# Latent attention: the key norm's sum of squares in one matmul over 96 rows

## The chip, the cores and the metric

The kernel is one program on one core of a Trainium2 chip. The metric is the time of one execution in device microseconds (us), the median of several executions. TensorE (PE, with its weight loads as PEld), VectorE (DVE), ScalarE (ACT), GpSimd (POOL) and the DMA queue of SyncE (SP) run side by side and wait for one another by semaphores.

## The reference

The input `x` (256 tokens by 1024) passes two layers of a first block and then two layers of a second one. The change lies in the second block, in the keys of its latent attention, twice, once per layer. Cut to that:

```python
c_q, c_kv, k_r, q_d, k_d, v_d = jnp.split(h @ w_in[l], split_at, axis=-1)
kv = (rmsnorm(c_kv, g_ckv) @ w_ukv).reshape(B, S, MLA_HEADS, MLA_NOPE + MLA_V)
k_nope, v = kv[..., :MLA_NOPE], kv[..., MLA_NOPE:]
k_rope = jnp.broadcast_to(k_rope_in[:, :, None, :], (B, S, MLA_HEADS, MLA_ROPE))
k = jnp.concatenate([k_nope, k_rope], axis=-1)
k = rmsnorm(k, g_kn)          # over 96 features: 64 of the head, 32 shared by all heads
k = jnp.concatenate([k[..., :MLA_NOPE], apply_rope_2(k[..., MLA_NOPE:], cos, sin)], axis=-1)
return dense_attention(q * (MLA_QK ** -0.5), k, v)
```

There are 8 heads. A key has 64 features of its own head and 32 (the rope part) that all heads share, and it is divided by the root of the mean square over all 96. In the same layer 8 heads of a dilated attention work on `q_d`, `k_d`, `v_d`; then come the output projection and a feed-forward part.

## The kernel before

All activations lie with features on the partitions and tokens along the free dimension, T = 256 tokens. Weights are streamed in pieces of up to 1 MB: SP loads a piece into one of three `raw` buffers, ACT copies it to a rounded high part `wh`, DVE subtracts to get the low part `wl` (`split`), and each product of the large matmuls (`gemm`, L1316) is taken three times, high by high, high by low, low by high.

The order of the work is set by hand. `plan_program` runs through the whole computation once in Python and writes a list of steps. Each engine's program walks that list and issues its own part of each step (the functions of the same name in the tensor, scalar, vector and gpsimd programs). Buffers come from pools handed out first in, first out: 8 PSUM banks, 8 temporaries `tmp` of 128x512, and a few smaller ones. A buffer that is given back carries the events after which it may be written, and whoever takes it next waits for them. So a buffer that is held longer leaves fewer for the others, and the order of the pool decides who waits for whom.

In a layer of the second block, the steps around the change are these.

- `lora1` (planned at L1057, ACT at L1659): ACT squares the three banks with the latent query and the latent key (`sq3`). The third bank also holds, in rows 64 to 95, the raw rope part of the keys; ACT squares that into `sqkr` (L1665, 32x256), and copies it scaled by the gain into `xg`. After it ACT has the next weight split.
- `lora2`: TensorE sums the squares by matmuls with a matrix of ones, ACT forms the reciprocal roots, and DVE and ACT write the normalised latents `cqn` and `ckn` in five steps, each through a temporary `u`. At its end DVE rotates the rope part of the keys into `krr`.
- Then six pieces of the dilated heads' projections (`dil_piece`), two of the queries (`queries`), each with head norms `hn1` and `hn2`, and from the fourth on, between them, the dilated attention itself (`heads("d")`: scores `sc2`, `exp2`, `wt2`, transposes `turn2`, values `val2`).
- `mla_proj` then projects the keys in four head pairs, hp = 0 to 3. For one pair `mla_k1` makes the 64 own features of both heads in one bank (12 matmuls, two heads side by side in the free dimension, 2 x 256), and ACT squares rows 0 to 63 into a temporary `sq`. One turn of the loop later, `mla_k2` (L1472) sums the squares over the features: one matmul with ones over rows 0 to 63 of `sq` (64x512), and two over rows 64 to 95 of `sqkr` (32x256), one for each head, all adding up in one bank `nb`. ACT takes logarithm and exponential (`rsqrt`), DVE multiplies into `k2` in two instructions (L1935, L1937), and the scores of these two heads may start.
- The steps of `mla_proj` are woven with those of the dilated heads (pair 0) and of the latent heads (pairs 1 to 3), so on TensorE a pair's `mla_k2` stands between scores and the next pair's `mla_k1`.

The trace gives matmuls of all small kinds the line L1351. A matmul on 4-byte numbers has two records in the trace, so the one over 64x512 is "x2", and the two over 32x256 are "x4". In shapes such as 64*96, the first number is the rows used (the contraction), the second the columns.

Of the kernel before, what the change touches and what calls it, by code (L numbers as in the profile page):

```python
# [11 lines left out]
ACT = mybir.ActivationFunctionType  # L12
# [4 lines left out]
T = 256  # L17
# [137 lines left out]
class Memory:  # L155
    def __init__(self, nc, banks):
# [78 lines left out]
        r2 = area(reg_off)  # L235
# [6 lines left out]
        self.kd = r2("kd", [P, 4, T])  # L242
        self.vd = r2("vd", [P, 2, 512])
        self.krr = r2("krr", [96, T])
        self.sqkr = r2("sqkr", [96, T])
        assert r2.end() <= b1_off
        rx = area(ctx_off)
        self.E2 = [rx(f"e2_{i}", [P, 512]) for i in range(2)]
# [10 lines left out]
class Plan:  # L259
# [15 lines left out]
    def ev(self, sem, by=1):  # L275
        self.count[sem] = self.count.get(sem, 0) + by
        return Ev(sem, self.count[sem])

    def step(self, name, **data):
        self.order.append((name, {k: as_now(v) for k, v in data.items()}))  # L280
# [96 lines left out]
def plan_program(M, pieces):  # L377
    p = Plan(M, pieces)
    ev, step, banks, tmps, stats, take = p.ev, p.step, p.banks, p.tmps, p.stats, p.take
# [57 lines left out]
    t_c, t_cs, z = ev("ld_c", 16), ev("csil"), ev("zero")  # L437
# [489 lines left out]
    for s in "cx":  # L927
        hd = ffn1(0, s, ht[s], ffn_step)
        nn, t = ffn_down("dn1", 0, s, hd, mvec(0, s, 5), t_mod[(0, 2)], [], True)
# [86 lines left out]
    n, t = ffn_down("dn1", 1, "x", hd, mvec(1, "x", 5), t_mod[(1, 2)], [], True)  # L1016
# [6 lines left out]
    for l in range(2):  # L1023
        a = H["x"]
        toks = n.finish(M.V(("an", l)), None, a, hfree["x"], [t, t_vec])
        rf = list(region_free)
        dil = {}

        def dil_piece(j):
# [11 lines left out]
            else:  # L1041
# [10 lines left out]
        f = take(("in2", l, 2))  # L1052
        bc = banks.get()
        tc = p.gemm(f, 8, 160, [(0, P, 0, bc), (64, 96, T, bc)], a, toks)
        sq3, xg = [tmps.get() for _ in range(3)], tmps.get()
        a3, k_sq, z, k_g = [ev("lsq") for _ in range(3)], ev("lsq"), ev("zero"), ev("lsq")
        step("lora1", l=l, bk=(ba, bb, bc), tk=(ta, tb, tc), sq3=sq3, sq_free=[q.free for q in sq3], xg=xg,  # L1057
             xg_free=xg.free, rf=rf, a3=a3, k_sq=k_sq, z=z, k_g=k_g)
        dil_piece(0)
        nq, nkv, br, rq, rk = banks.get(), banks.get(), banks.get(), None, None  # L1060
        tq, tkv, t_sw = ev("mm"), ev("mm"), ev("mm")
# [5 lines left out]
        r_free = (rq.free, rk.free)  # L1067
# [26 lines left out]
        cq_toks, ck_toks, t_krr = c_toks[0:3], c_toks[3:5], t_kr[2]  # L1094
# [47 lines left out]
            yield  # L1142

        def k_part(hp, f):
            b, sq = banks.get(), tmps.get()
            t, x = ev("mm"), ev("ksq")
            step("mla_k1", hp=hp, f=f, b=b, free=b.free, ck_toks=ck_toks, sq=sq, sq_free=sq.free, t=t, x=x)

            def rest():
                nb, r = banks.get(), tmps.get()  # L1150
                tn, t_l, t_r, o1, o2 = ev("mm"), ev("ln"), ev("rs"), ev("k2"), ev("k2")
                step("mla_k2", l=l, hp=hp, b=b, sq=sq, x=x, k_sq=k_sq, nb=nb, nb_free=nb.free, r=r, r_free=r.free,
                     t_krr=t_krr, tn=tn, t_l=t_l, t_r=t_r, o1=o1, o2=o2, rf=rf)
                tmps.give(sq, tn)
                banks.give(nb, t_l)
                banks.give(b, o1)
                tmps.give(r, o2)
                k_toks.append(o2)
            return rest, t
# [78 lines left out]
        bk = []  # L1238
# [12 lines left out]
        for ch in range(2):  # L1251
            f = take(("out2", l, 0, ch))
            for i in range(2):
                tk = p.gemm(f, 4, 512, [(P * (2 * i + j), P, T * j, bk[2 * ch + i]) for j in range(2)], H["c"],
                            mix_toks, first=False, done=i == 1)
                t = add_resid(s, bk[2 * ch + i], tk, 2 * ch + i, None, None, [])
# [58 lines left out]
def tensor_program(pe, on, M, plan):  # L1315
# [34 lines left out]
    def mm(out, lhsT, rhs, start, stop):  # L1350
        return pe.matmul(out, lhsT, rhs, start=start, stop=stop, skip_group_check=True)  # L1351
# [117 lines left out]
                ins = mm(o, whi[:, k, c], M.ckn[1][:, k, :], False, k == 1)  # L1469
        ins.then_inc(*on.inc(t))  # L1470

    def mla_k2(sq, x, k_sq, nb, nb_free, tn, **_):  # L1472
        on.wait_ge(x, nb_free, k_sq)
        mm(nb.t[0:96, :], M.ones[0:64, 0:96], sq.t[0:64, :], True, False)
        for i in range(2):
            ins = mm(nb.t[0:96, T * i:T * i + T], M.ones[64:96, 0:96], M.sqkr[64:96, :], False, True)
        ins.then_inc(*on.inc(tn))

    def sc2(mla, h, b, free, ready, t, **_):
        on.wait_ge(ready, free)  # L1480
# [30 lines left out]
def scalar_program(act, on, M, plan, io):  # L1511
# [3 lines left out]
    def fn(out, in_, func, scale=1.0, bias=0.0, accum=None):  # L1515
        if func in (ACT.Ln, ACT.Exp):
            if table[0] != LOG_SET:
                act.preload_act_table_set(LOG_SET)
            table[0] = LOG_SET
        elif func not in (ACT.Copy, ACT.Identity, ACT.Square):  # L1520
            table[0] = func
        if accum is None:
            return act.activation(out, in_, func, bias=bias, scale=scale)  # L1523
        return act.activation(out, in_, func, bias=bias, scale=scale, accum_out=accum)
# [131 lines left out]
        on.wait_ge(t, b1_free)  # L1656
        fn(M.bias[:, h, :], o.t[:, :], ACT.Copy).then_inc(*on.inc(x))

    def lora1(l, bk, tk, sq3, sq_free, xg, xg_free, rf, a3, k_sq, z, k_g, **_):  # L1659
        for i, n in enumerate((512, 512, T)):  # L1660
            on.wait_ge(tk[i], sq_free[i])
            fn(sq3[i].t[:, 0:n], bk[i].t[:, 0:n], ACT.Square).then_inc(*on.inc(a3[i]))
        on.wait_ge(rf)
        kr = bk[2].t[64:96, T:2 * T]
        fn(M.sqkr[64:96, :], kr, ACT.Square).then_inc(*on.inc(k_sq))  # L1665
        on.wait_ge(xg_free)
        fn(xg.t[64:96, 0:T], kr, ACT.Copy, scale=M.vcol(("gmk", l), 0, 64, 96)).then_inc(*on.inc(k_g))

# [19 lines left out]
    def mla_k2(nb, r, r_free, tn, t_l, t_r, **_):  # L1688
        on.wait_ge(tn, r_free)
        rsqrt(r, nb.t[0:96, :], 512, 1.0 / 96, t_l, t_r)  # L1690
# [552 lines left out]
```

## Time and profile before

| | |
|---|---|
| median of 3 runs | 1815.62 us (1813.46 to 1820.35) |
| the profiled execution | 1810.96 us |
| its span, first to last instruction | 1809.2 us |
| its mean granted TensorE clock | 0.975 of full speed |
| TensorE busy, matmuls | 1702.9 us, 94% |
| TensorE busy, weight loads | 1534.6 us, 85% |
| VectorE busy | 1062.7 us, 59% |
| ScalarE busy | 886.4 us, 49% |
| GpSimd busy | 192.7 us, 11% |
| DMA | 299.12 MB, mean 165 GB/s |

Busy shares are means over the span. The second block's two layers begin at about 1070 us and 1440 us, and each has its latent keys about 90 to 135 us later. Start times in the rows are us from the start of the span. "idle before" in brackets is the time that the engine stood before the row, with the instruction that ended it.

### The profile page before, as it was taken

The numbers are of one execution on the slowest core, as the hardware profiler recorded it, in microseconds if no ns is written. First come the engines' busy times: TensorE is split into PE (matmuls) and PEld (weight loads), VectorE is DVE, ScalarE is ACT, GpSimd is POOL, SyncE is SP. The second block draws the span as 40 slices with busy tenths as digits, with TensorE's granted clock in tenths as the row PEclk, the third lists the DMA queues.
The fourth block names the chain that finished last, engine by engine and source line by source line (L and its number), as shares of the span: only waits on it lengthen the run. The fifth ranks groups of instructions, "written<-read, shape, count | busy, mean of one in ns | idle before, by whom it ended". The sixth has DMA issues, their size and how long they took to land. (4 is left out here: it accounts for less than half of the span.)

```text
span 1809.2 us, 30326 instructions
## 1 busy us (share of the span) xinstructions
PE 1702.9 (94%) x12896; PEld 1534.6 (85%) x12896; DVE 1062.7 (59%) x1472; ACT 886.4 (49%) x1190; POOL 192.7 (11%) x138
## 2 busy tenths in 40 slices
PE   5899988999999999988999999998999999989999
PEld 2777657999999999956899989667999996679999
DVE  2498556544455445976644455746776457457763
ACT  3334556544354434555544445645654456455552
POOL 1140000122002210300122100000111000000110
PEclk7999989999999999999999999999999999899999
DMA  8234546456546544472465443303455443025552
GB/s 365 94 140 163 210 175 233 187 211 240 189 153 216 186 175 158 171 263 79 142 217 186 176 155 129 115 24 110 173 186 193 171 143 117 3 91 191 188 195 103
DMA packets 45110, 299.12 MB, mean 165 GB/s; under 512 B 5216, under 2 KB 7360, under 8 KB 11696
## 3 DMA queue, kind: packets, MB, share of 16 engines
q1 hardware_dynamic: 44304, 295.65, 45.6%
q8 instruction: 102, 1.67, 0.4%
q0 software_dynamic: 240, 0.79, 0.1%
q10 hardware_dynamic: 432, 0.75, 0.1%
q14 instruction: 32, 0.26, 0.0%
HBM read 296.10 MB, written 1.06 MB: 164 GB/s over the span
## 5 line engine op out<-in xcount | busy, mean ns | idle before, releaser
L1747 DVE TENSOR_TENSOR wl<-raw,wh 128x2048 fp32r<-128x2048 f32 (+3 forms) x236 | 529.0, 2242 | 520.9 <-ACT wh L1523 470.4
L1523 ACT ACTIVATE wh<-raw 128x2048 fp32r<-128x2048 f32 (+3 forms) x236 | 437.1, 1855 | 260.7 <-PE bank L1331 163.9
L1326 PE MATMUL bank<-hx_hi,wh 128*128 128x256 f32 x1920 | 548.1, 285 | 16.3 <-ACT hx_hi L1523 9.7
L1329 PE MATMUL bank<-hx_hi,wl 128*128 128x256 f32 x1920 | 539.2, 281 | 2.9 <-DVE wl L1747 2.9
L1331 PE MATMUL bank<-hx_lo,wh 128*128 128x256 f32 x1920 | 539.1, 281 | 0.0
L1326 PEld LDWEIGHTS bank<-hx_hi,wh 128*128 128x128 f32 x1920 | 362.8, 189 | 24.2 <-issue 19.3
L1329 PEld LDWEIGHTS bank<-hx_hi,wl 128*128 128x128 f32 x1920 | 362.4, 189 | 8.3 <-DVE wl L1747 4.2
L1331 PEld LDWEIGHTS bank<-hx_lo,wh 128*128 128x128 f32 x1920 | 362.6, 189 | 0.4 <-DVE hx_lo L1739 0.2
L1326 PE MATMUL bank<-hid_hi,wh 128*128 128x256 f32 x880 | 246.0, 280 | 0.0
L1329 PE MATMUL bank<-hid_hi,wl 128*128 128x256 f32 x880 | 245.7, 279 | 0.0
L1331 PE MATMUL bank<-hid_lo,wh 128*128 128x256 f32 x880 | 245.7, 279 | 0.0
L1326 PE MATMUL bank<-hc_hi,wh 128*128 128x256 f32 x752 | 218.1, 290 | 6.5 <-issue 3.0
L1329 PE MATMUL bank<-hc_hi,wl 128*128 128x256 f32 x752 | 214.1, 285 | 7.0 <-DVE wl L1747 7.0
L1331 PE MATMUL bank<-hc_lo,wh 128*128 128x256 f32 x752 | 213.9, 284 | 1.5 <-DVE hc_lo L1854 0.8
L1331 PEld LDWEIGHTS bank<-hid_lo,wh 128*128 128x128 f32 x880 | 165.2, 188 | 0.0
L1326 PEld LDWEIGHTS bank<-hid_hi,wh 128*128 128x128 f32 x880 | 165.1, 188 | 0.0
L1329 PEld LDWEIGHTS bank<-hid_hi,wl 128*128 128x128 f32 x880 | 164.9, 187 | 0.0
L1326 PEld LDWEIGHTS bank<-hc_hi,wh 128*128 128x128 f32 x752 | 145.2, 193 | 19.8 <-issue 19.5
L1329 PEld LDWEIGHTS bank<-hc_hi,wl 128*128 128x128 f32 x752 | 145.0, 193 | 8.2 <-DVE wl L1747 7.8
L1523 ACT ACTIVATE tmp<-bank,vec 128x256 f32<-128x256 f32 (+3 forms) x188 | 105.8, 586 | 92.7 <-PE bank L1331 52.4
L1331 PEld LDWEIGHTS bank<-hc_lo,wh 128*128 128x128 f32 x752 | 145.4, 193 | 2.1 <-DVE hc_lo L1854 1.0
L2029 POOL TENSOR_TENSOR hid_lo<-tmp,hid_hi 128x512 fp32r<-128x512 f32 x33 | 91.6, 2777 | 350.0 <-ACT hid_hi L1523 350.0
(211 smaller groups left out, 1982.2 us busy)
## 6 DMA issues: line engine op xcount, KB each, us to landing
raw<-in_wts SPq DMA_DIRECT2D x258, 1024.0 KB, 4.8
raw<-in_wts SPq DMA_DIRECT2D x20, 768.0 KB, 4.0
raw<-in_wts SPq DMA_DIRECT2D x4, 576.0 KB, 3.5
tmp<-tscr SPq DMA_DIRECT2D x16, 128.0 KB, 4.2
raw<-in_wts SPq DMA_DIRECT2D x2, 640.0 KB, 3.8
xTc<-in_ctxT SPq DMA_DIRECT2D x1, 1024.0 KB, 10.8
xTx<-in_xT SPq DMA_DIRECT2D x1, 1024.0 KB, 8.6
out_x<-xTx POOLq DMA_DIRECT2D x3, 256.0 KB, 5.5
```

The costliest lines, as they stand in the source:

```text
L1326: pe.matmul(out, hi[:, k, c:c + m], x_hi, start=first and k == 0 and o == 0, stop=False, skip_group_check=True)
L1329: pe.matmul(out, lo[:, k, c:c + m], x_hi, start=False, stop=False, skip_group_check=True)
L1331: ins = pe.matmul(out, hi[:, k, c:c + m], x_lo, start=False, stop=last and k == nk - 1, skip_group_check=True)
L1523: return act.activation(out, in_, func, bias=bias, scale=scale)
L1747: tt(M.wl[k][:, 0:ne], M.raw[f["r"]][:, 0:ne], M.wh[k][:, 0:ne].bitcast(F32), ALU.subtract).then_inc(*on.inc(f["tlo"]))
L2029: tt(lo, y.t[:, :], hi.bitcast(F32), ALU.subtract).then_inc(*on.inc(t[1]))
```

## The change

The squares of the rope part are no longer in a tensor of their own. In `lora1` two temporaries, `kq`, are taken from the pool, and ACT writes the squares twice into each, once per head of a pair, into rows 64 to 95 (32x512, the source read twice by a broadcast). The four head pairs use these two buffers in turn as their `sq`: ACT still writes the own squares into rows 0 to 63, and one matmul over rows 0 to 95 (96x512) replaces the three. The buffers stay out of the pool until the third and fourth pair are done with them. A pair's own squares wait for the matmul of the pair two before.

```diff
-        self.sqkr = r2("sqkr", [96, T])
...
         sq3, xg = [tmps.get() for _ in range(3)], tmps.get()
-        a3, k_sq, z, k_g = [ev("lsq") for _ in range(3)], ev("lsq"), ev("zero"), ev("lsq")
+        kq = [tmps.get() for _ in range(2)]
+        a3, k_sq, z, k_g = [ev("lsq") for _ in range(3)], [ev("lsq"), ev("lsq")], ev("zero"), ev("lsq")
...
+        kq_use = [[t] for t in k_sq]
...
-            b, sq = banks.get(), tmps.get()
+            b, sq = banks.get(), kq[hp % 2]
...
-            step("mla_k1", hp=hp, f=f, b=b, free=b.free, ck_toks=ck_toks, sq=sq, sq_free=sq.free, t=t, x=x)
+            step("mla_k1", hp=hp, f=f, b=b, free=b.free, ck_toks=ck_toks, sq=sq, sq_free=kq_use[hp % 2], t=t, x=x)
...
-                tmps.give(sq, tn)
+                kq_use[hp % 2] = [tn]
+                if hp > 1:
+                    tmps.give(sq, tn)
...
-    def mla_k2(sq, x, k_sq, nb, nb_free, tn, **_):
-        on.wait_ge(x, nb_free, k_sq)
-        mm(nb.t[0:96, :], M.ones[0:64, 0:96], sq.t[0:64, :], True, False)
-        for i in range(2):
-            ins = mm(nb.t[0:96, T * i:T * i + T], M.ones[64:96, 0:96], M.sqkr[64:96, :], False, True)
-        ins.then_inc(*on.inc(tn))
+    def mla_k2(sq, x, nb, nb_free, tn, **_):
+        on.wait_ge(x, nb_free)
+        mm(nb.t[0:96, :], M.ones[0:96, 0:96], sq.t[0:96, :], True, True).then_inc(*on.inc(tn))
...
-        on.wait_ge(rf)
         kr = bk[2].t[64:96, T:2 * T]
-        fn(M.sqkr[64:96, :], kr, ACT.Square).then_inc(*on.inc(k_sq))
+        for i in range(2):
+            on.wait_ge(kq_free[i])
+            fn(kq[i].t[64:96, :].rearrange("p (a t) -> p a t", a=2), kr.unsqueeze(1).to_broadcast([32, 2, T]),
+               ACT.Square).then_inc(*on.inc(k_sq[i]))
```

No instruction changes its place against the others on any engine: eight times two matmuls go from TensorE, and twice one ACT instruction becomes two. The numbers behind the names of buffers are those of the tensors; without `sqkr` those of later tensors are one less (`e_0_124` is `e_0_123`), and the temporaries rotate in another order. `cst` holds the matrix of ones, and L1354 is the line that was L1351.

TensorE, first layer, pair 0, behind the scores of a dilated head (`kd`,`qd`), before:

```order
L1351 MATMUL bank<-pT_0_126,vd 64x256 x2
L1494 MATMUL bank<-cst,e_0_124 128x128 x4
L1351 MATMUL bank<-kd,qd 128x256 x2
L1351 MATMUL bank<-tmp_84,cst 96x512
L1351 MATMUL bank<-sqkr,cst 96x256 x2
L1351 MATMUL bank<-ckn_hi,wh_58 128x256
```

and of the changed kernel:

```order
L1354 MATMUL bank<-pT_0_125,vd 64x256 x2
L1494 MATMUL bank<-cst,e_0_123 128x128 x4
L1354 MATMUL bank<-kd,qd 128x256 x2
L1354 MATMUL bank<-tmp_83,cst 96x512
L1354 MATMUL bank<-ckn_hi,wh_58 128x256
```

The two matmuls on `sqkr` are gone, all else stands as it stood. An order row gives the shape of the output, so that the matmul on `tmp` reads 96x512 in both, with 64 rows of input before and 96 now.

TensorE, first layer, pair 1, behind the scores of the first two latent heads (`k_117`,`q_116`), before:

```order
L1351 MATMUL bank<-pT_0_126,vd 64x256 x2
L1351 MATMUL bank<-k_117,q_116 128x256 x4
L1351 MATMUL bank<-tmp_82,cst 96x512
L1351 MATMUL bank<-sqkr,cst 96x256 x2
L1351 MATMUL bank<-ckn_hi,wh_58 128x256
```

and of the changed kernel:

```order
L1354 MATMUL bank<-pT_0_125,vd 64x256 x2
L1354 MATMUL bank<-k_117,q_116 128x256 x4
L1354 MATMUL bank<-tmp_79,cst 96x512
L1354 MATMUL bank<-ckn_hi,wh_58 128x256
L1354 MATMUL bank<-ckn_hi,wl_61 128x256
```

Here the matmul stands behind one over 96 rows, and pairs 2 and 3 read the same but for what is next to them.

ACT, first layer, `lora1`, from the squares of the three banks to the square of the next projection, before:

```order
L1523 ACTIVATE tmp_84<-bank 128x512
L1523 ACTIVATE tmp_80<-bank 128x256
L1523 ACTIVATE sqkr<-bank 32x256
L1523 ACTIVATE tmp_82<-bank,vec 32x256
L1523 ACTIVATE wh_58<-raw_55 128x2048
L1523 ACTIVATE tmp_83<-bank 128x512
```

and of the changed kernel:

```order
L1523 ACTIVATE tmp_84<-bank 128x512
L1523 ACTIVATE tmp_80<-bank 128x256
L1523 ACTIVATE tmp_83<-bank 32x512
L1523 ACTIVATE tmp_79<-bank 32x512
L1523 ACTIVATE tmp_82<-bank,vec 32x256
L1523 ACTIVATE wh_58<-raw_55 128x2048
L1523 ACTIVATE tmp_81<-bank 128x512
```

`tmp_83` and `tmp_79` are the two `kq` buffers. They are the ones that the next head norm took before, and it takes the two behind them now.

## Rows read from the trace of the kernel before

**Rows 1.** The page, busy time of the engines.

```profile
PE 1702.9 (94%) x12896; PEld 1534.6 (85%) x12896; DVE 1062.7 (59%) x1472; ACT 886.4 (49%) x1190; POOL 192.7 (11%) x138
```

**Rows 2.** Groups by line and form, all of the span: the squares' matmuls, ACT's square.

```profile
L1351 PE MATMUL bank<-sqkr,cst 32*96 32x256 f32 x32 | 12.5, 525 | 0.0
L1351 PE MATMUL bank<-tmp,cst 64*96 64x512 f32 x16 | 10.8, 758 | 0.0
L1523 ACT ACTIVATE tmp<-bank 64x512 f32<-64x512 f32 x8 | 4.7, 587 | 5.5 <-PE bank L1351 5.5
```

**Rows 3.** Waits of TensorE, 1075 to 1235: us in total, times, longest.

```profile
PE bank L1494 <- DVE e L1735: 3.6, 2, 2.9
PE bank L1351 <- DVE k L1937: 1.4, 1, 1.4
```

**Rows 4.** Timeline of TensorE, pair 1: start, us, engine, line, what, count.

```profile
1187.23 1.10 PE L1351 MATMUL bank<-tmp,cst 64*96 64x512 f32 x2
1188.26 1.10 PE L1351 MATMUL bank<-sqkr,cst 32*96 32x256 f32 x4
1189.28 0.38 PE L1351 MATMUL bank<-ckn_hi,wh 128*128 128x256 f32 x1
...
1192.29 1.13 PE L1351 MATMUL bank<-k,q 96*128 96x256 f32 x4 [1.37 <-DVE k L1937]
```

**Rows 5.** Timeline of TensorE, scores of a dilated head, then query norms.

```profile
1134.10 1.13 PE L1351 MATMUL bank<-kd,qd 64*128 64x256 f32 x4
1135.16 3.67 PE L1351 MATMUL bank<-tmp,cst 96*96 96x512 f32 x8
1138.27 0.69 PE L1343 MATMUL bank<-wh,hx_hi 128*128 128x256 f32 x1
```

**Rows 6.** Timeline of TensorE, pair 0.

```profile
1169.63 0.48 PE L1351 MATMUL bank<-kd,qd 64*128 64x256 f32 x1
1169.64 0.84 PE L1351 MATMUL bank<-tmp,cst 64*96 64x512 f32 x1
...
1171.29 2.02 PE L1351 MATMUL bank<-sqkr,cst 32*96 32x256 f32 x4
1173.24 0.58 PE L1351 MATMUL bank<-ckn_hi,wh 128*128 128x256 f32 x1
```

**Rows 7.** Windows: us, busy of each engine (count), granted clock, DMA share, GB/s.

```profile
1170.20:1176.80 6.60, 6.60 (x23) 4.44 (x21) 3.98 (x9) 3.87 (x10) 0.00 (x0) 0.50 0.01 1
...
1194.00:1200.60 6.60, 6.60 (x23) 4.81 (x22) 2.28 (x5) 2.23 (x6) 0.00 (x0) 0.50 0.00 0
```

**Rows 8.** Timeline of ACT, pair 1.

```profile
1188.29 0.20 ACT L1524 ACTIVATION_READ_ACCUMULATOR e<-bank,st 128x1 f32 x1
1189.39 0.69 ACT L1523 ACTIVATE tmp<-bank,vec 96x512 f32<-96x512 f32 x1 [0.91 <-PE bank L1351]
```

**Rows 9.** Timeline of TensorE and DVE, pair 2.

```profile
1193.35 1.51 PE L1351 MATMUL bank<-tmp,cst 64*96 64x512 f32 x2
...
1196.73 0.58 PE L1351 MATMUL bank<-ckn_hi,wh 128*128 128x256 f32 x1
...
1199.00 0.68 DVE L1937 TENSOR_TENSOR k<-tmp,krr 32x512 f32<-32x512 f32 x1
...
1199.46 1.05 PE L1494 MATMUL bank<-cst,e 128*128 128x128 f32 x4
```

**Rows 10.** Timeline of ACT, DVE and TensorE, `lora1`.

```profile
1093.46 0.38 ACT L1523 ACTIVATE sqkr<-bank 32x256 f32<-32x256 f32 x1
...
1096.36 2.29 DVE L1747 TENSOR_TENSOR wl<-raw,wh 128x2048 fp32r<-128x2048 f32 x1 [4.41 <-ACT wh L1523]
...
1101.01 0.28 PE L1329 MATMUL bank<-hx_hi,wl 128*128 128x256 f32 x1
```

**Rows 11.** Timeline of ACT and DVE, end of `lora2` and the next head norms.

```profile
1108.73 0.42 DVE L1930 TENSOR_TENSOR krr<-krr,tmp 32x256 f32<-32x256 f32 x1
...
1110.82 0.68 ACT L1523 ACTIVATE tmp<-bank,vec 128x512 f32<-128x512 f32 x1
```

More of the change, by code:

```diff
@@ L1055, in plan_program @@
         sq3, xg = [tmps.get() for _ in range(3)], tmps.get()
-        a3, k_sq, z, k_g = [ev("lsq") for _ in range(3)], ev("lsq"), ev("zero"), ev("lsq")
+        kq = [tmps.get() for _ in range(2)]
+        a3, k_sq, z, k_g = [ev("lsq") for _ in range(3)], [ev("lsq"), ev("lsq")], ev("zero"), ev("lsq")
         step("lora1", l=l, bk=(ba, bb, bc), tk=(ta, tb, tc), sq3=sq3, sq_free=[q.free for q in sq3], xg=xg,
-             xg_free=xg.free, rf=rf, a3=a3, k_sq=k_sq, z=z, k_g=k_g)
+             xg_free=xg.free, a3=a3, kq=kq, kq_free=[q.free for q in kq], k_sq=k_sq, z=z, k_g=k_g)
+        kq_use = [[t] for t in k_sq]
         dil_piece(0)
@@ L1151, in rest @@
                 tn, t_l, t_r, o1, o2 = ev("mm"), ev("ln"), ev("rs"), ev("k2"), ev("k2")
-                step("mla_k2", l=l, hp=hp, b=b, sq=sq, x=x, k_sq=k_sq, nb=nb, nb_free=nb.free, r=r, r_free=r.free,
+                step("mla_k2", l=l, hp=hp, b=b, sq=sq, x=x, nb=nb, nb_free=nb.free, r=r, r_free=r.free,
                      t_krr=t_krr, tn=tn, t_l=t_l, t_r=t_r, o1=o1, o2=o2, rf=rf)
-                tmps.give(sq, tn)
+                kq_use[hp % 2] = [tn]
+                if hp > 1:
+                    tmps.give(sq, tn)
                 banks.give(nb, t_l)
@@ L1657, in bias, with lora1 @@
         fn(M.bias[:, h, :], o.t[:, :], ACT.Copy).then_inc(*on.inc(x))
-    def lora1(l, bk, tk, sq3, sq_free, xg, xg_free, rf, a3, k_sq, z, k_g, **_):
+    def lora1(l, bk, tk, sq3, sq_free, xg, xg_free, a3, kq, kq_free, k_sq, z, k_g, **_):
         for i, n in enumerate((512, 512, T)):
```

## The prediction

> **What bounds the kernel now.** I read the page first: TensorE is busy 94% of the span, DVE 59%, ACT 49% [rows 1], so time is TensorE's, and another engine counts only where TensorE stands and waits for it. Then the groups by form, to see what the edited matmuls cost: 12.5 us for those on `sqkr` and 10.8 us for those over 64 rows [rows 2], at 8 places, four head pairs in each of two layers. So all that is touched is about 23 us, 1.3% of the span. Then TensorE's waits in the first layer's stretch: the long ones are for DVE's weights of a softmax, 3.6 us in two waits, which no edit touches, and one of 1.4 us for DVE's `k`, which hangs on `mla_k2` [rows 3]. Last the timeline around each pair, and the granted clock. It is 0.50 (1.2 GHz in place of 2.4) in two stretches of at least 6.6 us, 1170.2 to 1176.8 and 1194.0 to 1200.6 [rows 7]. Pairs 0 and 2 fall into them, pairs 1 and 3 do not. The second layer has the same rows again 368.6 us later, pair for pair, to within 0.05 us (one set of them stands), so I work out one layer and double it.
>
> **Term 1, a pair at full clock (1 and 3).** TensorE goes from the first record of the 64-row matmul at 1187.23 to the first of the next step at 1189.28: 2.05 us, of which 1.03 up to the `sqkr` matmuls and 1.02 for these [rows 4]. The new form is in the trace already: the query norms are matmuls over 96 rows by 512, four of them in 8 records from 1135.16 to 1138.27, 3.11 us or 0.78 us each [rows 5]. Bounds for the new matmul at this place: 0.78 below, and 1.03 above, what the 64-row one takes until the next starts. I take 0.78, as row count and neighbours (96-row scores before it, 128-row matmuls behind) are nearest to that row. TensorE is freed of 2.05 - 0.78 = 1.27 us (1.02 by the other bound).
>
> For pair 1 not all of it arrives. The 1.37 us wait behind the pair [rows 4] is for a chain: matmul, ACT's logarithm at 1189.39, exponential, DVE's two multiplications, scores at 1192.29 [rows 4, 8]. The logarithm waited 0.91 us for TensorE. ACT's instruction before it is a read of the accumulator at 1188.29, and ACT starts the next about 0.1 us after such a start, so the logarithm can come 1.0 us earlier, not 1.27. The rest of the 1.27 becomes idle time of TensorE. Pair 1: 1.0 us (0.9 to 1.27).
>
> For pair 3 (same three rows, 1201.48 to 1203.53, again 2.05) TensorE goes on with values whose inputs are ready, and waits for nothing of this chain soon. Pair 3: 1.27 us (1.0 to 1.27).
>
> **Term 2, pair 2, at half clock.** From 1193.35 to 1196.73 the three matmuls take 3.38 us [rows 9], nearly all of it in the slow stretch [rows 7]. One might count 3.38 - 1.56, 1.8 us, as the gain. But the slow stretch is a stretch of time: what is saved in it is filled by later work that then runs slow too. So I count in full-clock time: 0.65 us before 1194.0 and 2.73/2 behind it make 2.01, against 0.78 for the new one, a gain of 1.23. Against it stands DVE's `k`, which ends at 1199.68, 2.95 us behind the matmuls' end, while TensorE, before it uses that `k`, has the next `mla_k1` (2.73 us) and transposes (1.05), until 1200.5 [rows 9]. If these move out of the slow stretch, they take half, 1.9 us, and a wait of up to 1 us appears; half inside gives about 0.3. Pair 2: 1.0 us (0.4 to 1.9).
>
> **Term 3, pair 0.** Here the change also takes something away. The scores of the dilated head use rows 64 to 127, the squares' matmul rows 0 to 63, into different banks, and they start 0.01 us apart [rows 6]: both are through at 1171.29, 1.66 us later, though alone the scores take 1.06 us at full clock and the other 1.03 [rows 5, 4]. A matmul over rows 0 to 95 overlaps rows 64 to 95 and can't run beside them. In full-clock time, before: 0.57 up to 1170.2 and 3.04/2 to 1173.24, 2.09 us. Now 1.06 + 0.78 = 1.84. Pair 0: 0.25 us (-0.1 to 0.5).
>
> The rows show that two matmuls share the array when rows and bank both differ (1169.63 and 1169.64), and that the 64-row and the 32-row ones of one bank go one after the other, 1.03 and 1.02 us [rows 4, 6]. The Trainium skill, "TensorE: Matmul & The Clock Gate", Part 3 (packing small matmuls), says that matmuls on separate row groups run concurrently; by that rule alone the three were one already, and the whole gain would be a loss at pair 0. "TensorEngine Tiling (Array Packing)", Gotcha 1 (PSUM pressure), adds that row tiles can't be in one bank at the same time, and the trace agrees with that at both places. The same page, Key Properties, says that a change of tiling mode drains the engine. By that rule three drains go with the two matmuls and a full-clock pair gives 1.27; by the columns alone, which are halved, it would be 1.03. The sum would be 7.0 us by the drains and 2 x (0 + 1.0 + 0.8 + 1.0) = 5.6 by the columns. The row of 0.78 for 96x512 against 1.03 for 64x512 speaks for the drains.
>
> **Sum.** A layer: 0.25 + 1.0 + 1.0 + 1.27 = 3.5 us; two layers 7.0 us. By the lower bounds 2 x 2.2 = 4.4, by the upper 2 x 4.9 = 9.8.
>
> **What I cost at nothing, and its cover.** ACT has one 32x256 square of 0.38 us less and two 32x512 ones more. Not in the trace; bounds are 0.38 (the 32x256 form) and 0.59 each (64x512) [rows 10, 2]. I take 0.59, the row with the same free size, so 0.8 us more in `lora1` of each layer. What it delays is the weight split behind it: DVE's low part, which waits for ACT's high part, ends at 1098.65, would end at 1099.45, and TensorE first reads it at 1101.01 [rows 10]. Uncovered it would cost 0.8 us a layer.
>
> Two temporaries less are in rotation for 110 us. I followed each changed wait to its event. In `lora2` the `u` steps now share one buffer, so DVE's next `u` waits for its own last result, about 0.1 us three times; the latents are used 20 us later. The head norms wait for events one norm later than before. The tightest is ACT's copy at 1110.82, now waiting for the end of `krr` at 1109.15, or 1109.45 with that delay [rows 11], 1.4 us early; the others have longer. The wait of a pair's own squares for the matmul two pairs before is older than 10 us. Nothing is queued behind an open wait. DMAs stay where they are; in these stretches their share is near zero [rows 7].
>
> Behind the pairs TensorE meets only chains that it starts itself (values, transposes, the norm), so the gain is carried to the end.
>
> The profiled execution has a span of 1809.2 us and 1.8 around it, 1810.96 in all; less 7.0 it is 1804.0. The median of the runs is 4.7 above the profiled one, and I put the gain on it: 1815.62 - 7.0 = 1808.6 us.
>
> **Rivals.**
>
> *A, the clock gives more.* The slow stretches follow TensorE's waits (the first comes after one of 2.9 us [rows 3]). A stretch of 6.6 us costs 3.3. If the steps, moved by some us, miss one slow stretch in each layer, the gain is 7.0 + 6.6, 1802.0 us. For it: earlier work shifts everything against the clock's changes. Against it: the 2.9 us wait stays as it is, and pair 1's wait grows by 0.27.
>
> *B, the gain is given back.* TensorE has less to do and waits a little more in this thin stretch, and one slow stretch in each layer lasts half as long again (1.65 us lost a layer), and perhaps the wait at pair 2 takes its full 1 us: 7.0 - 3.3 to 7.0 - 5.3, so 1811.9 to 1813.9 us. For it: 94% busy is a mean, and the waits of rows 3 all lie in this thin stretch. Against it: only 0.3 us of wait is added at pair 1.
>
> *C, slower.* The same mechanism at its worst: a further full slow stretch of 6.6 us (3.3 lost) behind each of the two that are there, in both layers, 4 x 3.3 = 13.2 against 7.0, +6.2 us: 1821.8. It decides from the third added stretch of these four. Against it: the rows on either side of the thin stretch are dense, and the waits added are 0.3 us.
>
> *D, buffers.* The pool of 6 makes ACT wait in a head norm and TensorE behind it, 1 us at each of 4 norms in a layer: 8 us, no gain, 1816.6. Against it stand the slacks above.
>
> *E, it doesn't do what it says.* If one matmul over 96 rows took the 2.05 us of the old three (which is where they would stand if the old ones shared the array already), the gain is nil, and pair 0 loses 1.06 + 2.05 - 2.09 = 1.0 a layer: 1817.7. The row of 0.78 is against it, and the 1.03 and 1.02 one behind the other [rows 4]. This is the outcome of the packing rule taken by itself.
>
> **Chances.** Forecast 0.62 (its own range 1805.5 to 1811.5), A 0.15, B 0.15, C 0.03, D 0.03, E 0.02. What the runs scatter (1813.46 to 1820.35) is as large as the effect, and adds 2 to 3 us to either side. The range is 1801.5 to 1814. About 0.5%, 9.1 us, is what a measurement can tell from no change: faster than 1806.5 takes A whole and the lower edge of the forecast, 0.25; slower than 1824.7 only a bad case of C, 0.03; within 0.5%: 0.72.
>
> **What would show it.** In the changed profile: no `sqkr`; at each pair one matmul "96*96 96x512 x2"; 0.8 us between its first record and the next step's at pairs 1 and 3 (not 1.0); at pair 0 `kd`,`qd` and it one behind the other; ACT's logarithm at pair 1 at once behind the accumulator read, and the wait for DVE's `k` 1.6 us instead of 1.37; the windows with clock 0.50 about as many. From the start of the second block's first layer to its end some 3.5 us less. It is wrong if the new matmul takes over 1.1 us at full clock, if a new wait for a temporary stands on ACT in the head norms, or if the time at 0.50 changes by more than 3.3 us a layer.

## The result and the profile after

The changed kernel takes 1798.95 us in the median of 5 runs (1794.97 to 1801.71), the kernel before 1815.62 (5 runs, 1808.19 to 1820.35): ratio 0.9918, 95% interval 0.9892 to 0.9944. Two later repeats give 0.9923 (0.9893 to 0.9952) and 0.9909 (0.9872 to 0.9945). Over all groups the mean falls from 1812.4 us (92 runs) to 1798.5 (17), 14.0 us. The forecast was 7.0.

Each run comes with its mean granted clock, so its time splits into two parts. The **clock loss** is (1 - mean clock) x span; the rest is the **time at full clock**. Before: loss 47.6 +- 0.5, rest 1764.9 +- 0.3 (standard errors). After: 39.4 +- 0.8 and 1759.0 +- 0.7. So 5.8 us are booked to the work and 8.2 to the clock. Below I use this split for every kernel. It is a way of booking: a low clock costs time only while TensorE works, so where TensorE waits in a slow stretch the loss is put somewhat too high and the rest too low.

The page, busy time of the engines, to be held against [rows 1]: TensorE is busy for 17 us less (work at half clock counts double in this figure), the others the same.

```profile
PE 1685.8 (94%) x12864; PEld 1526.0 (85%) x12864; DVE 1063.0 (59%) x1472; ACT 886.3 (49%) x1192; POOL 192.7 (11%) x138
```

Groups by form, against [rows 2]: `sqkr` is gone, and the new squares on ACT cost 0.58 us each, where I had assumed 0.59.

```profile
L1354 PE MATMUL bank<-tmp,cst 96*96 96x512 f32 x48 | 24.7, 639 | 0.0
L1523 ACT ACTIVATE tmp<-bank 32x512 f32<-32x512 f32 x4 | 2.1, 581 | 0.0
```

Timeline of TensorE at pair 1 (answers to [rows 4]). From the scores' first record to the second record of the next projection there were 1189.51 - 1185.31 = 4.20 us before; now 2.81. That is 1.39 less (forecast 1.27). I measure to the second record because the first one of the next projection now starts 0.46 us behind the new matmul's first and runs beside it; from first record to first, the measure of the forecast's 0.8, TensorE is freed of 2.05 - 0.46 = 1.59 us.

```profile
1184.64 1.99 PE L1354 MATMUL bank<-k,q 96*128 96x256 f32 x8
1186.47 1.02 PE L1354 MATMUL bank<-tmp,cst 96*96 96x512 f32 x2
1186.93 0.68 PE L1354 MATMUL bank<-ckn_hi,wh 128*128 128x256 f32 x1
1187.45 0.28 PE L1354 MATMUL bank<-ckn_hi,wl 128*128 128x256 f32 x1
...
1190.60 1.13 PE L1354 MATMUL bank<-k,q 96*128 96x256 f32 x4 [1.69 <-DVE k L1939]
```

ACT there (answers to [rows 8]). The logarithm no longer waits for TensorE; it starts right behind the read of the accumulator, as forecast, and so TensorE's wait for `k` grows from 1.37 to 1.69 us.

```profile
1187.62 0.20 ACT L1524 ACTIVATION_READ_ACCUMULATOR e<-bank,st 128x1 f32 x1
1187.71 0.68 ACT L1523 ACTIVATE tmp<-bank,vec 96x512 f32<-96x512 f32 x1
```

Timeline of TensorE at pair 0 (answers to [rows 6]): `kd`,`qd` and the sum one behind the other.

```profile
1168.54 0.66 PE L1494 MATMUL bank<-cst,e 128*128 128x128 f32 x4 [2.86 <-DVE e L1737]
1169.12 2.03 PE L1354 MATMUL bank<-kd,qd 64*128 64x256 f32 x4
1171.08 2.02 PE L1354 MATMUL bank<-tmp,cst 96*96 96x512 f32 x2
```

TensorE's waits from 1075 to 1235 (answers to [rows 3]). There are three waits for the softmax weights where there were two; the new one, 0.57 us at 1208.37, is where part of the gain of pairs 2 and 3 went. The six waits for ACT's `pT`, 4.1 us in all, are the same before and after.

```profile
PE bank L1494 <- DVE e L1737: 4.2, 3, 2.9
PE bank L1354 <- ACT pT L1523: 4.1, 6, 0.7
PE bank L1354 <- DVE k L1939: 1.7, 1, 1.7
```

Windows (columns as in [rows 7]). The clock (0.5 is the level of 1.2 GHz) is low at pair 0 as before, but the stretch at pair 2 is gone (a shorter one, 3.4 us, comes at 1244); in the second layer both have half their length.

```profile
1169.50:1176.30 6.80, 6.80 (x21) 4.40 (x21) 3.99 (x9) 4.07 (x10) 0.00 (x0) 0.52 0.02 4
1190.60:1200.60 10.00, 10.00 (x58) 7.73 (x59) 6.26 (x15) 6.11 (x15) 0.00 (x0) 1.00 0.01 2
1534.70:1538.10 3.40, 3.40 (x14) 2.69 (x12) 2.08 (x6) 1.80 (x6) 0.00 (x0) 0.54 0.00 0
1555.20:1558.60 3.40, 3.40 (x18) 3.40 (x17) 1.85 (x3) 1.90 (x3) 0.00 (x0) 0.54 0.00 0
```

The kernel before had in the second layer:

```profile
1538.90:1545.70 6.80, 6.80 (x24) 4.57 (x21) 3.98 (x9) 3.81 (x10) 0.00 (x0) 0.52 0.01 2
1562.80:1569.60 6.80, 6.80 (x24) 5.08 (x24) 2.62 (x7) 2.44 (x6) 0.00 (x0) 0.52 0.00 0
```

I followed DVE's instructions, which are the same in both, through the two traces (before minus after, us), and took half of the half-clock time out ("of it clock"; a minus means longer):

| stretch of the first layer | shorter by | of it clock | the rest |
|---|---|---|---|
| 1155.4 to 1180.4 (pair 0) | 0.16 | 0 | 0.16 |
| to 1192.5 (pair 1) | 1.03 | 0 | 1.03 |
| to 1215.1 (pairs 2 and 3) | 5.19 | 3.4 | 1.77 |
| to 1263.3 | -1.41 | -1.7 | 0.29 |
| sum | 4.97 | 1.7 | 3.25 |

The second layer has 7.2 in this profile and 6.4 in the two repeats, of these 3.4 clock and 3.0 the rest. The first profile also has 3.7 us less between 1701 and 1806, far behind the change; in the repeats and in every kernel below that stretch is within 0.02 us of before. That was one execution, not the change.

So the traces put 3.4 + 1.7 = 5.1 us of the gain down to the clock in the two layers, the same in all three profiles of the changed kernel, against one of before: 13.7 us of loss there before, 8.5 after. The runs say 8.2 +- 1.0. The other 3 us I can't place. Before 1130 us, where the kernels hardly differ, the loss is between 23.9 and 32.4 us in the 18 profiles of this document, so a single profile's total says little.

### The profile page after: what moved, and what is told of

Read it like the earlier page. It is cut to its first block and busy times, and to the rows that moved or that the text cites. A ratio compares the mean times of both kernels' runs of the same rounds, so it can differ in the third digit from the quotient of the medians.

```text
span 1793.1 us, 30262 instructions
## 1 busy us (share of the span) xinstructions
PE 1685.8 (94%) x12864; PEld 1526.0 (85%) x12864; DVE 1063.0 (59%) x1472; ACT 886.3 (49%) x1192; POOL 192.7 (11%) x138
## 3 DMA queue, kind: packets, MB, share of 16 engines
HBM read 296.10 MB, written 1.06 MB: 166 GB/s over the span
## 5 line engine op out<-in xcount | busy, mean ns | idle before, releaser
L1329 PEld LDWEIGHTS bank<-hx_hi,wh 128*128 128x128 f32 x1920 | 364.0, 190 | 23.9 <-issue 19.7
```

What stands on the lines that cost most here:

```text
L1329: pe.matmul(out, hi[:, k, c:c + m], x_hi, start=first and k == 0 and o == 0, stop=False, skip_group_check=True)
```

## The experiments

All are edits of the changed kernel unless it says otherwise. "Loss" and "full" are means with standard errors over n runs, in us; the last column is the clock loss in one profile from 1500 to 1660, the stretch of the second layer. The kernels were run in four groups of four, in the order of the table, each with its own runs of before: loss 46.3, 46.4, 48.4 and 50.7, errors 0.8, 0.7, 1.0 and 1.8. A difference of 2 us between kernels of different groups is therefore weak.

| kernel | n | ratio (95%) | loss | full | 2nd layer |
|---|---|---|---|---|---|
| before | 92 | 1 | 47.6 +- 0.5 | 1764.9 +- 0.3 | 6.8 |
| after_again | 6 | 0.9923 (0.9893-0.9952) | 40.1 +- 0.9 | 1757.8 +- 1.0 | 3.4 |
| three_on_kq | 12 | 0.9988 (0.9969-1.0008) | 44.3 +- 1.1 | 1765.7 +- 0.5 | 5.1 |
| twice | 12 | 0.9964 (0.9945-0.9983) | 40.0 +- 1.0 | 1765.1 +- 0.6 | 3.4 |
| pair0_three | 12 | 0.9957 (0.9939-0.9976) | 44.1 +- 0.6 | 1759.3 +- 0.6 | 5.1 |
| fill | 8 | 0.9941 (0.9921-0.9961) | 39.6 +- 0.8 | 1761.6 +- 1.1 | 3.4 |
| fill_before | 12 | 0.9995 (0.9978-1.0013) | 44.3 +- 1.3 | 1767.0 +- 0.6 | 13.7 |
| wide | 6 | 0.9927 (0.9900-0.9954) | 39.5 +- 1.6 | 1758.7 +- 0.9 | 3.4 |
| own_only | 11 | 0.9947 (0.9930-0.9964) | 44.2 +- 0.5 | 1758.7 +- 0.5 | 6.8 |
| pair0_one | 12 | 0.9971 (0.9951-0.9992) | 42.5 +- 1.4 | 1765.5 +- 0.5 | 6.8 |
| p0three_l0 | 6 | 0.9927 (0.9899-0.9956) | 42.0 +- 2.1 | 1758.8 +- 0.9 | 3.4 |
| p0three_l1 | 6 | 0.9933 (0.9907-0.9958) | 42.3 +- 1.1 | 1759.4 +- 0.9 | 6.8 |
| barrier_p0 | 12 | 0.9958 (0.9940-0.9976) | 42.8 +- 0.9 | 1762.5 +- 0.7 | 5.1 |
| after_third | 6 | 0.9909 (0.9872-0.9945) | 38.3 +- 2.0 | 1760.4 +- 1.2 | 3.4 |
| p0_own | 9 | 0.9924 (0.9895-0.9954) | 43.4 +- 0.6 | 1757.7 +- 1.0 | 6.8 |
| p0_own_barrier | 7 | 0.9918 (0.9886-0.9951) | 40.1 +- 0.8 | 1759.8 +- 1.0 | 5.1 |
| p0_barrier | 7 | 0.9914 (0.9880-0.9948) | 39.3 +- 0.8 | 1759.8 +- 0.7 | 3.4 |

### What of the change is it: the first group

`after_again`, no edit.

> The changed kernel once more, unaltered, as the yardstick of this group. Theory M (the gain is that of the matmuls, some 1.5 us at a pair, plus the clock, whose second half-speed stretch beside pairs 2 and 3 goes): 0.992 of the kernel before, 14 to 17 us less, and again only one stretch at clock 0.50 between 1160 and 1215 us. Rival L (that stretch went by luck of this one profile, and 4 us of the drift in the last feed-forward part too): ratio nearer 0.996, stretches of clock 0.50 at other places, and the drift in the last 170 us of the span not there.

The gain stands. There is one stretch at clock 0.50 between 1160 and 1215 again, and only the tail's 3.7 us were chance.

`three_on_kq`:

```diff
-        mm(nb.t[0:96, :], M.ones[0:96, 0:96], sq.t[0:96, :], True, True).then_inc(*on.inc(tn))
+        mm(nb.t[0:96, :], M.ones[0:64, 0:96], sq.t[0:64, :], True, False)
+        for i in range(2):
+            ins = mm(nb.t[0:96, T * i:T * i + T], M.ones[64:96, 0:96], sq.t[64:96, T * i:T * i + T], False, True)
+        ins.then_inc(*on.inc(tn))
```

> The changed kernel with its two buffers and its two ACT squares, but the sum taken by three matmuls again, one over rows 0 to 63 and two over rows 64 to 95 of the buffer. Theory M: the whole gain comes from TensorE, so this is the kernel before again, ratio 0.999 to 1.001. Rival B (fewer temporaries in rotation, other waits on ACT, a different order of events are part of it): ratio 0.995 to 0.998. If ACT's added 0.8 us a layer cost something: 1.001.

At full clock it is the kernel before, 1765.7. So buffers and ACT cost and give nothing, as I had booked them.

`twice` issues the 96-row matmul two times.

> The changed kernel with the 96-row matmul issued twice, each starting its bank anew, so that the sum is the same and TensorE passes 1024 columns a pair as before, but with no change to 32 rows and none of the row groups that the three had. Theory M with drains (what is saved at a pair is the switch of rows as much as the columns): two in a row cost 2 x 0.5 us, against 2.05 for the three, so some two fifths to half of the gain stays: ratio 0.996. Rival C (columns alone): time of the kernel before, 0.999 to 1.000. By the time of 0.78 a matmul of the query norms two would be 1.56 at a pair.

By "full" the columns win (1765.1, no gain left), but the loss stays at 40: by this split the whole 0.9964 is the clock's. Its one profile shows less of that, 11.9 us of loss in the two layers against 13.7 before. Timeline of TensorE in `twice`, pair 1:

```profile
1188.14 1.88 PE L1354 MATMUL bank<-tmp,cst 96*96 96x512 f32 x4
1189.45 0.68 PE L1354 MATMUL bank<-ckn_hi,wh 128*128 128x256 f32 x1
1189.97 0.28 PE L1354 MATMUL bank<-ckn_hi,wl 128*128 128x256 f32 x1
```

The second matmul adds (1189.97 - 1188.14) - (1187.45 - 1186.47) = 0.85 us. The three took 1.39 more than one, so 0.85 of it is columns. The other 0.54 I put down to the switches between row groups; it is what is left over and was not measured by itself, and the full time of `twice` shows no gain from it.

`pair0_three` (the three matmuls of above stand under `if hp == 0`):

> The changed kernel, but pair 0 of each layer sums by three matmuls from the same buffer, the first of which can run beside the dilated head's scores in rows 64 to 127. By the prediction's term for pair 0, 0.25 us a layer, this is 0.5 us slower than the changed kernel (0.992 becomes 0.9925). In the profile of the changed kernel pair 0 takes 3.6 to 4.0 us from the start of the scores to the first matmul of the next projection, against 3.6 before, so the rival says that it gains or loses nothing, or gains 0.3 us a layer here (0.9915). If the clock reacts to where pair 0 ends, the stretches at 0.50 change instead, by steps of 1.7 us.

Its full time is that of the changed kernel, but the loss is 44.1, 4 us more. With my own term for pair 0, worth 0.5 us in the two layers, this was the surprise of the group. In its profile the two layers lose 10.2 us, 1.7 more than in the changed kernel, and the stretch before 1130 us has 32.4, the highest of all; what the twelve runs lost where, no trace shows.

### The clock: filler, width, rows

`fill` (in `turn2` of the dilated head 4) and `fill_before`, the same on the kernel before:

```diff
-        on.wait_ge(r, free)
+        on.wait_ge(free)
+        for _i in range(fill):      # 8
+            mm(b.t[:, 0:P], M.ones, M.ident, True, True)
+        on.wait_ge(r)
```

> The changed kernel with eight useless 128x128 matmuls of ones and identity, in each layer, issued in TensorE's wait of 2.86 us for DVE's weights at 1168.5 (their bank is overwritten by the transposes behind them). They need an estimated 1.8 to 2.2 us and so fit into the wait. Theory K (what the clock costs in this stretch is set by what TensorE does just before, and the idle time calls for the half-speed stretch that follows it at 1169.5): the stretch of 6.8 at pair 0 goes or shrinks to 3.4 in both layers, and the kernel is 3.4 to 6.8 us faster than the changed one, ratio 0.988 to 0.990. Rival P (the stretches come by chance and position): same time as the changed kernel, 0.992 to 0.993, and the stretch stays.

> The kernel before with the same eight useless matmuls in the same wait of each layer. Theory K: the stretches of 6.8 at pair 0, and perhaps the ones at pair 2 behind them, shrink, 3.4 to 10 us less, ratio 0.995 to 0.998; if it gets most of what the change got from the clock, then what the change won beyond its direct 6.5 us was the clock's, not the matmuls'. Rival P: 1.000.

Neither theory holds. Filling the long wait does put the drop off, but not away: TensorE runs on at full clock into the next waits, and the drop comes there. In the first layer it then lasts longer (10.2 us for 6.8), in the second as long as in the changed kernel (3.4). Timeline and window of `fill`:

```profile
1164.63 2.05 PE L1354 MATMUL bank<-cst 128*128 128x128 f32 x16
1167.56 0.66 PE L1497 MATMUL bank<-cst,e 128*128 128x128 f32 x4 [0.89 <-DVE e L1740]
...
1174.70 1.08 PE L1354 MATMUL bank<-pT,vd 128*64 128x256 f32 x4 [1.39 <-ACT pT L1526]
1177.59 1.12 PE L1497 MATMUL bank<-cst,e 128*128 128x128 f32 x4 [1.81 <-DVE e L1740]
```

```profile
1166.00:1176.80 10.80, 7.50 (x41) 4.73 (x39) 6.94 (x18) 6.08 (x16) 0.00 (x0) 0.99 0.00 1
1176.80:1187.00 10.20, 8.03 (x21) 4.62 (x22) 2.24 (x9) 2.94 (x8) 0.00 (x0) 0.51 0.00 0
```

In the changed kernel these two waits are 0.69 and 0.73: work at half clock covers them. `fill_before` even has 23.9 us at half clock from 1544.7 on, in its one profile; over its twelve runs the loss is 44.3, no higher than before.

`wide` takes `M.ones[0:96, :]` and `nb.t[:, :]`.

> The changed kernel with the sum's matmul over all 128 columns of ones in place of 96 (rows 96 to 127 of its bank get a sum that nobody reads). The same 512 columns pass, so the direct time is that of the changed kernel within 0.1 us. If the clock goes by how much of the array is at work as well as by time, the half-speed stretches shrink and it is 1 to 3 us faster (0.991); if only by whether TensorE is busy, no difference (0.9925).

No difference in either part: with 32 more columns of the array the loss is 39.5 +- 1.6 against 40.1 +- 0.9.

`own_only` takes `M.ones[0:64, 0:96]` and `sq.t[0:64, :]`. It leaves the rope part out of the sum, so its keys are not those of the reference.

> The changed kernel with the rope part left out of the sum: one matmul over rows 0 to 63 alone, so the keys' norm is taken over the own 64 features only. Theory M by columns: the number of rows costs nothing, and this is the changed kernel's direct time at pairs 1 to 3, within 0.1 us. At pair 0 it can run beside the dilated scores in rows 64 to 127: if that overlap is worth something, TensorE reaches the next projection 0.5 to 0.8 us earlier than the changed kernel there, as the prediction's term 3 assumes (it priced the overlap at about 0.8); if not, at the same time.

Full time as the changed kernel, loss 44.2. At full clock, pair 0 of its second layer shows scores and sum wholly side by side, 1.06 us for both (timeline of TensorE):

```profile
1533.80 0.48 PE L1354 MATMUL bank<-kd,qd 64*128 64x256 f32 x1
1533.81 0.67 PE L1354 MATMUL bank<-tmp,cst 64*96 64x512 f32 x1
...
1534.86 0.39 PE L1354 MATMUL bank<-ckn_hi,wh 128*128 128x256 f32 x1
```

One behind the other at full clock, in the second layer of `fill`, the two take 1.06 + 0.54. Yet no time at the end comes of that half microsecond: the full times, 1758.7 and 1759.0, are equal within 0.9.

So after these eight kernels, with before, the loss of the runs went in two bands: 39.5 to 40.1 where the sum of pair 0 can't run beside the scores, 44 to 48 where it can.

### Pair 0 by itself

`pair0_one` is `three_on_kq` with one matmul at `hp == 0`; `p0three_l0` and `p0three_l1` have the three at pair 0 of one layer; `barrier_p0` has them behind `mm(nb.t[:, 0:P], M.ones, M.ident, True, True)`.

> The changed kernel with the one matmul over 96 rows at pair 0 alone; pairs 1 to 3 sum by three matmuls from the buffers. Theory O (what the change won from the clock comes from pair 0, where the sum no longer runs beside the dilated scores in rows 64 to 127): the time lost to the clock falls from 46 to about 40 us although almost no work is taken away, the time at full clock stays that of the kernel before (1765), 1805 in all, ratio 0.9965. Rival P (less work at pairs 1 to 3 moves the stretches): loss 44 to 46, ratio 0.999 to 1.000.

The full time is that of before, 1765.5, as expected: the direct gain is all of pairs 1 to 3. The loss is 42.5, between the two forecasts (before had 48.4 in this group). Its profile has both second stretches, which speaks for the rival, and in both layers together it loses 13.7 us, exactly as before; none of the 5.9 us that the runs gained on their own group is to be seen there:

```profile
1192.70:1199.50 6.80, 6.80 (x24) 5.24 (x23) 2.97 (x7) 3.24 (x8) 0.00 (x0) 0.52 0.00 0
1561.40:1568.20 6.80, 6.80 (x24) 5.29 (x23) 2.97 (x7) 3.19 (x7) 0.00 (x0) 0.52 0.00 0
```

> The changed kernel with the three matmuls at pair 0 of the first of the two layers alone. In the profiles so far the clock costs 3.4 us in the second layer's stretch (1500 to 1660) in all five kernels without the overlap and 5.1 to 13.7 in the five with it, while in the first layer both kinds have 5.1 to 8.5. By that, theory O2 (it acts in the second layer only): as the changed kernel, loss 40 us, ratio 0.9925. Rival (it acts in both): loss 42, ratio 0.9937.

> The changed kernel with the three matmuls at pair 0 of the second layer alone. Theory O2: loss 44 us, as with the overlap in both, ratio 0.995 and over 3.4 us of clock loss between 1500 and 1660. Rival (both layers): loss 42, ratio 0.9937.

Both 42, with errors of 2.1 and 1.1, in a group whose before had 48.4. That would fit a cost of 2 us in each layer, but it can't rule out "second layer only". The ratios lean that way (0.9927, as forecast for it, and 0.9933), and so do the profiles: the first layer loses 5.1 us with the overlap and without it, in every kernel that has one matmul at pairs 1 to 3 and no filler but `barrier_p0`. Which layer it is stays open.

> The changed kernel with the three matmuls at pair 0 of both layers, but behind one useless 128x128 matmul over all 128 rows, which stands between them and the dilated scores, so that they can't run side by side. Theory O (the overlap itself calls for the lower clock): loss back at 40 us although the three matmuls are there; at full clock 1 to 2 us a layer more than the changed kernel, 1801 to 1803. Rival F (the form of the matmuls, 32 and 64 rows, is what does it): loss 44, so 1805 to 1807.

42.8 +- 0.9: nearer to rival F's 44 than to O's 40, and the mean time, 1805.3, is in F's range. Its profile loses 13.7 us in the two layers, as much as before. So with the overlap gone, the three matmuls at pair 0 still cost something.

### Overlap, form or shift

`p0_own` takes the 64-row matmul alone at `hp == 0`, and so leaves the rope part out of that pair's norm; `p0_own_barrier` puts the useless matmul ahead of it; `p0_barrier` puts it ahead of the 96-row one.

> The changed kernel unaltered, as the yardstick of this group. Theory O: 0.992 to 0.9925, clock loss 40 us (11 runs so far), 1758 us at full clock, 3.4 us lost between 1500 and 1660 in its profile.

> The changed kernel, but at pair 0 of each layer the sum is taken over the own 64 rows alone (the rope part is left out of that pair's norm), in one matmul over rows 0 to 63 that can run beside the dilated scores. There is no 32-row matmul in it. Theory O (it is the two matmuls side by side): clock loss 44, 1758 at full clock, 1802, 0.995. Rival F (the 32-row matmuls with the array three quarters empty lowered the clock): loss 40, 0.992.

> The same 64-row matmul at pair 0 behind one useless 128x128 matmul over all rows, so that nothing runs beside the scores. Theory O: the loss is back at 40 us, and at full clock it is some 0.3 to 0.6 us a layer over the changed kernel, 1799, 0.993. Rival S (any shift of this place by about 1 us does it, whatever runs side by side): loss anywhere from 40 to 44, not ordered by overlap.

> The changed kernel with its 96-row matmul at pair 0, behind the same useless matmul. Nothing runs side by side, before or after, so this is the price of the useless matmul alone. Theory O: loss 40, 0.3 to 0.6 us a layer at full clock, 1799, 0.993. Rival S: the loss moves by 2 us or more, as the place is half a microsecond later.

Loss 43.4 with overlap, 40.1 with the barrier, 39.3 with the barrier on the changed kernel, 38.3 without. By the loss that goes by theory O: neither the 32-row matmuls nor the shift is needed, and the overlap alone adds 3.3 +- 1.0 to it. By time it is weaker. The ratio of `p0_own`, 0.9924, is what rival F had forecast (0.992) and not O (0.995): its full time is 2.1 +- 1.4 us lower than that of `p0_own_barrier`, so all that is left at the end is 1.2 +- 0.9 us. The other pairs with and without the overlap in one group differ more in time: `pair0_three` against `after_again` 5.5 +- 1.0, `own_only` against `wide` 4.7 +- 1.1. By full time all four kernels of this group lie within 2.7 us, where an error is 1.0. The profile of `p0_own`, second layer, shows how (timeline of TensorE, then a window):

```profile
1529.55 0.66 PE L1498 MATMUL bank<-cst,e 128*128 128x128 f32 x4 [2.87 <-DVE e L1741]
1530.13 0.48 PE L1354 MATMUL bank<-kd,qd 64*128 64x256 f32 x1
1530.15 0.67 PE L1354 MATMUL bank<-tmp,cst 64*96 64x512 f32 x1
...
1536.68 1.08 PE L1354 MATMUL bank<-pT,vd 128*64 128x256 f32 x4 [2.01 <-ACT pT L1527]
1539.58 1.12 PE L1498 MATMUL bank<-cst,e 128*128 128x128 f32 x4 [1.82 <-DVE e L1741]
```

```profile
1538.50:1548.70 10.20, 7.75 (x21) 4.35 (x22) 2.49 (x10) 2.94 (x8) 0.00 (x0) 0.51 0.01 2
```

And `p0_own_barrier` at the same place:

```profile
1530.34 0.66 PE L1499 MATMUL bank<-cst,e 128*128 128x128 f32 x4 [2.87 <-DVE e L1742]
1530.92 1.13 PE L1354 MATMUL bank<-kd,qd 64*128 64x256 f32 x4
...
1540.50 1.08 PE L1354 MATMUL bank<-pT,vd 128*64 128x256 f32 x4 [0.69 <-ACT pT L1528]
1542.31 0.66 PE L1499 MATMUL bank<-cst,e 128*128 128x128 f32 x4 [0.73 <-DVE e L1742]
```

```profile
1532.30:1539.10 6.80, 6.80 (x20) 3.92 (x19) 3.77 (x9) 3.06 (x8) 0.00 (x0) 0.52 0.00 0
```

Each layer takes one of two courses. **Early**: the clock is low right around pair 0, for 3.4 to 10.2 us of solid work, and the waits behind it are short. **Late**: it stays high there (but for 3.4 us in one layer of `own_only`), TensorE arrives early, waits 0.7 to 2.0 and then 1.8 us for ACT and DVE, and the clock is low after or during these waits, in most for 10.2 us. Over all profiles without the filler, 7 of 12 layers with the overlap went late (both of `three_on_kq` and `own_only`, one each of `p0_own`, `p0three_l0`, `p0three_l1`), and 0 of 20 layers without it. In those 20, pair 0 begins anywhere from 1165.2 to 1169.1 and from 1529.2 to 1538.1 us, so its position alone doesn't send a layer late. The kernel before went early in both layers of its one profile. What a late layer costs more is seen in the second layer only: 5.1 to 6.8 us of loss, against 3.4 to 5.1 in the early ones with one or two matmuls at pairs 1 to 3.

The second stretch, at pair 2, goes by pairs 1 to 3. In early layers it is there, 6.8 us long, in 4 of 4 with three matmuls at these pairs (before, `pair0_one`). With one matmul it is absent in 15 of 19 and 3.4 us long in 4; in 14 of the 15 a stretch of 3.4 us comes instead, 72 to 75 us behind the one at pair 0.

## Why the prediction was wrong

**What bounds the kernel, the costs at nothing, buffers:** right. No new wait for a temporary, and none of TensorE's waits from 1075 to 1235 is for DVE's low part of a weight. Rival D is out by `three_on_kq` (full time unchanged), and rival E by 2.81 against 4.20 us at pair 1.

**Term 1:** right. 1.03 us arrived at pair 1 (forecast 1.0), with the wait at 1.69 (1.6), and TensorE's own saving was 1.39 (1.27), or 1.59 by the first records, which stand 0.46 us apart and not 0.8.

**Terms 1 and 2, pairs 2 and 3:** 1.77 at full clock instead of 2.27. The new wait of 0.57 us for DVE's weights at 1208.37 took it; I had said that nothing is late behind pair 3.

**Term 3:** 0.16 (0.25) at full clock, but this was the wrong thing to price there.

**Sum:** 3.25 and 2.98 us in the layers, 6.2 (forecast 7.0); 5.8 +- 0.8 by the split of the runs. The mechanism and the size of the direct gain were right. At pair 1 the columns are 0.85 of 1.39; the 0.54 left over for the drains is not shown by itself.

**The step that failed** is in term 2: "the slow stretch is a stretch of time", what is saved in it "is filled by later work that then runs slow too", and with it the last line of what would show it, "the windows with clock 0.50 about as many". I took the low clock as fixed. In the two layers the time at half clock fell from 27.3 us to 17.1 in all three profiles of the changed kernel, which is 5.1 us; by the runs the clock was worth 8.2 +- 1.0 us, more than all terms together. The prediction's own sign of being wrong, over 3.3 us a layer less or more at 0.50, came true in both layers: 3.4 and 6.8 us less.

That is rival A (6.6 us, to which I gave 0.15), and its price and time (1802.0) were near, but not its cause. I argued for A by a mere shift of position. The experiments point to two causes. One is the work at pairs 1 to 3: the half-clock stretch of 6.8 us at pair 2 was there in 4 of 4 early layers with three matmuls, and in none with one; whether less work or its earlier time does it was not separated. The other is the overlap at pair 0, with which 7 of 12 layers took the late course.

How much each is worth is not shown. A two by two of the runs has loss 39.4 with one matmul everywhere, 44.1 with three at pair 0 only, 42.5 with three at pairs 1 to 3 only, 44.3 with three everywhere from the same buffers. By it pair 0 is worth 2 to 5 us and pairs 1 to 3 between 0 and 3. The profiles of the same four kernels lose 8.5, 10.2, 13.7 and 12.0 us in the two layers. By these pairs 1 to 3 are worth 2 to 5 and pair 0 at most 2, the other way round. One profile of a kernel is little, and the runs are of different groups. The 3.3 +- 1.2 us between `three_on_kq` and before stay unexplained; the before runs of that very group had 46.3 +- 0.8, which leaves 2.0 +- 1.4.

The overlap that I booked as a small loss of the change (1.06 beside 1.03 us) was no loss at the end. Where a layer went late, what it saved was given back as a wait, and the runs with it lost 3 to 5 us more to the clock than those without it in their own group. Against A, I wrote that the 2.9 us wait stays and pair 1's grows. Both happened, and the clock did not care; the sum of waits was no guide to it.

The level was off too: 1815.62, a median of three, lies 3.2 above the mean of 92.

**Open:** where the 3 us between the clock's 8.2 of the runs and 5.1 of the profiles lie; before has one profile. Why the clock stays high at the long wait more often with two matmuls side by side. With the sum half a microsecond later (`p0_barrier`) it did not, nor with a wider matmul (`wide`). Also how the three matmuls at pair 0 cost clock without the overlap (`barrier_p0`, 42.8 against 39.3 for `p0_barrier`), and how the gain is split between pair 0 and pairs 1 to 3, where runs and profiles disagree.

No kernel tried beats the changed one; `wide` and `p0_barrier` are within its error.

## What to carry to other kernels

Split every time into the part at full clock and (1 - mean clock) x span before explaining it: here a profile's rows forecast the first to about 1 us, and the second moved by more. Look for the second in the traces too, stretch by stretch, and in more than one of each kernel: one profile of before was too few here. In a thin stretch, where TensorE waits for a chain through ACT and DVE anyway, neither running matmuls side by side nor filling the wait bought time here, since TensorE only came to the next wait sooner. Price the half-clock stretches next to an edit as things that can go, with a chance to match: here they went when work beside them went.

## What the hardware showed

- A matmul over 96 rows and 512 columns on 4-byte numbers behind another over 96 rows costs 0.85 us (`twice`); ahead of the next 128-row one, from its first record to that one's second, it takes 0.98 us, against 1.25 us for the one over 64 rows in `own_only` (1187.17 to 1188.42). Fewer rows were not cheaper.
- The clock's low stretches in the two layers lasted 3.4, 6.8, 10.2 and once 23.9 us. Eight 128x128 matmuls in a wait of 2.86 us moved a drop from 1169 to 1177 (6.8 us before, 10.2 then) and in the second layer from 1534 to 1542 (3.4 us both times).
- Runs of one kernel differ mostly by the clock: over the first 29 runs of before, time and clock loss go together with a correlation of 0.85.
